# Splitting a weight load whole instead of in halves, in a two-block network on one core

## The chip, the cores and the metric
One core of one Trainium2 chip runs the whole program. The time is the device time of one execution in microseconds (us); a smaller one is better. Engines: TensorE (PE; PEld is its weight loading), VectorE (DVE), ScalarE (ACT), GpSimd (POOL), SyncE (SP, which issues the weight loads).

## What is computed
Two network blocks on 256 tokens of width 2048, in fp32. Cut to its products and stages:
```python
mod = silu(c) @ ada_w + ada_b                       # 96 columns of 128: shifts, scales, gains
h = rmsnorm(x) * (1 + sc1) + sh1
z = h @ w_in                                        # q, k, v, gates, recurrent and merge parts
o_a = compressed, selected and window attention     # 16 heads in 4 groups
o_b = gelu(ly) * rg_lru(conv(lx))
x += g1 * ((sigmoid(ga) * (o_a @ proj_a) + sigmoid(gb) * (o_b @ proj_b)) @ w_out)
x += g2 * ((gelu(conv(gate)) * val) @ ffn_down)     # gate, val = rmsnorm(x).. @ ffn_up
x = rmsnorm(x)
# second block: window attention of 4 head groups, a diagonal state-space scan in 8 rounds,
# a gated unit (w_glu), two projections, merge and output product
```

## The kernel before
**Products in three terms.** Each weight product is done in a reduced form of fp32 three times: high part of the weight with high and with low part of the activation, and low part of the weight with the high one. A weight must therefore be split: `whi` is a rounded copy, made by ScalarE (`split_act`, L1064 to L1069); `wlo` is the weight less `whi`, made by VectorE (`split_dve`, L1071 to L1077), in the place of the raw weight.

**Loads and units.** SyncE loads 1 MB at a time (4 x 128 rows by 512 columns, 2048 elements a partition) into a ring `wraw` of RAW = 5 slots. A load serves two *units* of TensorE, each 24 matmuls of 256 columns (1024 elements a partition of the weight). The table of groups (`groups()`, L52) sets the order of all units; most groups (512 output columns) have 8. The group of the gates alone has one unit and one load, of 768 elements. Between the loads, in the prologue and behind the second and fourth load of many groups up to the first part of the feed-forward stage, stand 96 modulation loads (`ada`): VectorE alone multiplies such a load (L1051) and frees its slot. A weight load's slot is free when TensorE ends its second unit. The ring is filled strictly in order (L1440 to L1458).

**Splits.** `whi` is a ring of HI = 6 halves; a half is made in one instruction on each of the two engines, LEAD = 5 units ahead of its use: at unit u the engines split unit u + 5, and ScalarE waits until TensorE has ended unit u - 1 (L1068). The first eight units are split in the prologue, a load behind each quarter of the first norm.

**Everything else** is written as jobs, generators whose steps all engines walk through in the same order. `walk` (L1413) gives each engine at each unit first its part of the unit (TensorE the matmuls, ScalarE and VectorE the split) and then the steps of the jobs due there. An engine's queue is in order, so a step stands behind the split of its unit. The jobs that matter here: `evac` (L1132, takes a group's result out of PSUM), `nsa` (L413, one head group of the first attention, over the 8 units of the next group; the last over 16), `norm2` (L1298, which stands before the steps of a unit, between two groups), `ssm_tables` (L819), `attention2` (L691, 8 units a head group) and `ssm` (L918, 10 units a round).

The lines that set the lead:
```python
        def unit(g, gr, u, n):
            if FIRST <= u + LEAD < N_UNITS:
                split_dve(dve, u + LEAD)
```
Of the kernel before, what the change touches and what calls it, by code (L numbers as in the profile page):

```python
# [6 lines left out]
F32 = mybir.dt.float32  # L7
F32R = mybir.dt.float32r
ACT = mybir.ActivationFunctionType
ALU = mybir.AluOpType  # L10
AX = mybir.AxisListType

P = 128
# [7 lines left out]
FFC = FF // P  # L21
CB = 512
RAW = 5
HI = 6
LEAD = 5


VEC_SIZES = [("ada_b", 96), ("norm1_g", 16), ("norm2_g", 16), ("final_g", 16), ("norm_w_2", 16),
# [73 lines left out]
def build_program(nc, ctx, xT, vecs, cvec, W, small, outT):  # L102
    base = 16640

    def put(name, at, shape, dt=F32):
        size = 4
        for n in shape[1:]:
            size *= n
        assert base + at + size <= nc.sbuf_usable_end, name
        return nc.alloc_sbuf_tensor_at(name, list(shape), dt, offset=base + at)  # L110
# [4 lines left out]
    K = 1024  # L115


    z0, z1, z2, rM, rW = 0, 32 * K, 64 * K, 96 * K, 112 * K
    rWh = rW + RAW * 8 * K
    rC = rWh + HI * 4 * K  # L120
    rT = rC + 8 * K
    rS = rT + 8 * K
    h1, m1 = put_pair("h1", z0, DC), put_pair("m1", z0, DC)
# [2 lines left out]
    hid = put_pair("hid", z0, 24)  # L126
    res = put("res", rM, [P, DC, T])
    wraw = put("wraw", rW, [P, RAW, 2048])
    wlo = put("wlo", rW, [P, RAW, 2, 1024], F32R)
    whi = put("whi", rWh, [P, HI, 1024], F32R)  # L130
    cb = put("cb", rC, [P, D])
    t1 = put("t1", rT, [P, 4, T])
    t2 = put("t2", rT + 4 * K, [P, 4, T])
# [83 lines left out]
    hi_ready, lo_ready, pe_units, ada_done = sem("hi_ready"), sem("lo_ready"), sem("pe_units"), sem("ada_done")  # L217
# [14 lines left out]
    GR, of = groups()  # L232
    U0, U1 = [], []
# [5 lines left out]
    N_UNITS = at  # L239
    SLOTS, HEAD = [], []  # L240
    unit_slot = {}
    behind = {}
    for g, gr in enumerate(GR):
        for s in range(gr.slots):
            per = gr.units // gr.slots
            if g == 0:
                HEAD.append(range(len(SLOTS), len(SLOTS) + 8))
                SLOTS += [("ada", col + c) for c in range(4 * s, 4 * s + 4) for col in (16, 0)]
            for n in range(per):
                unit_slot[U0[g] + s * per + n] = (len(SLOTS), n)  # L250
            SLOTS.append(("w", g, s, U0[g] + (s + 1) * per))
            for col in gr.ada.get(s, ()):
                behind.setdefault(U0[g] + (s + 1) * per - 1, []).append(len(SLOTS))
                SLOTS.append(("ada", col))
    N_ADA = 0
    ada_no = {}
# [4 lines left out]
    where = []  # L261
# [785 lines left out]
    def ada(dve, z):  # L1047

        slot, col = z % RAW, SLOTS[z][1]
        dve.wait_ge(w_loaded[slot], 16 * (z // RAW + 1))  # L1050
        ve.scalar_tensor_tensor(out=wraw[:, slot, :], in0=wraw[:, slot, :], scalar=1.0, in1=cb[:, :], op0=ALU.mult,  # L1051
                                op1=ALU.mult, accum_out=mod[:, col:col + 1]).then_inc(ada_done, 1)
        if col == 47:
            with_bias(32, 16)
        elif col == 63:
            with_bias(48, 32)
            gain_of(scA, 0, 64, "norm2_g", DC)
        elif col == 95:
            with_bias(80, 16)

    def width(u):
        return 768 if where[u][0].mode == "GATES" else 1024

    def split_act(act, u):  # L1064
        (z, half), r, w = unit_slot[u], u % HI, width(u)
        act.wait_ge(w_loaded[z % RAW], 16 * (z // RAW + 1))
        if u >= HI:
            act.wait_ge(pe_units, u - HI + 1)  # L1068
        sc.activation(whi[:, r, 0:w], wraw[:, z % RAW, 1024 * half:1024 * half + w], ACT.Copy).then_inc(hi_ready, 1)  # L1069

    def split_dve(dve, u):  # L1071
        (z, half), r, w = unit_slot[u], u % HI, width(u)
        dve.wait_ge(hi_ready, u + 1)
        ve.tensor_tensor(wlo[:, z % RAW, half, 0:w], wraw[:, z % RAW, 1024 * half:1024 * half + w],  # L1074
                         whi[:, r, 0:w].bitcast(F32), ALU.subtract).then_inc(lo_ready, 1)
        for z in behind.get(u, ()):
            ada(dve, z)  # L1077

    def split_unit(j, u):
        if j.me == "act":  # L1080
            split_act(j.eng, u)
        if j.me == "dve":
            split_dve(j.eng, u)

    FIRST = 8

    def prologue(j):
        me, ins = j.me, None
        if me == "act":
            j.eng.wait_ge(c_in, 16)  # L1090
            ins = sc.activation(cb[:, :], cb[:, :], ACT.Silu)
        c_ready = j.give("act_to_dve", "act", ins)
        if me == "act":
            j.eng.wait_ge(consts_in, 16)
            sc.activation(ltmp[:, 3, :], V("lru_lambda", 0, DC), ACT.Abs)
            sc.drain()
            ins = sc.activation(ltmp[:, 3, :], ltmp[:, 3, :], ACT.Exp, scale=-1.0)
        j.sync("act_to_dve", "act", "dve", ins)
        if me == "dve":
            j.eng.wait_ge(consts_in, 16)  # L1100
            log_decay()
            ve.tensor_tensor(scB[:, :], V("final_g", 0, DC), V("norm_w_2", 0, DC), ALU.mult)
            ve.drain()
        j.take("act_to_dve", "dve", c_ready)
        for b in range(4):
            if me == "dve":
                for z in HEAD[b]:
                    ada(j.eng, z)
                with_bias(16 + 4 * b, 4)
                with_bias(4 * b, 4)  # L1110
                gain_of(scA, 4 * b, 16 + 4 * b, "norm1_g", 4) if b else None
            if b == 0:
                for _ in norm1(j):
                    pass
                if me == "dve":
                    gain_of(scA, 0, 16, "norm1_g", 4)
            normed(j, "h1", h1, 4 * b, rstd[:, :], scA, 0)
            split_unit(j, 2 * b)
            split_unit(j, 2 * b + 1)

    def merged(j):

# [342 lines left out]
    @block.scalar  # L1465
    def _(act):
        j = Job("act", act)
        prologue(j)

        def unit(g, gr, u, n):  # L1470
            if FIRST <= u + LEAD < N_UNITS:
                split_act(act, u + LEAD)

        walk(j, unit)

    @block.vector
    def _(dve):
        j = Job("dve", dve)
        ve.memset(ones[:, :], 1.0)
        ve.memset(halves[:, :], 0.0)  # L1480
        ve.drain()
        ve.memset(halves[0:64, 0:64], 1.0)
        ve.memset(halves[64:128, 64:128], 1.0)
        ve.drain().then_inc(c_made, 1)
        prologue(j)
        dve.wait_ge(consts_made, 1)

        def unit(g, gr, u, n):
            if FIRST <= u + LEAD < N_UNITS:
                split_dve(dve, u + LEAD)  # L1490

        walk(j, unit)

    @block.tensor
    def _(pe):
        j = Job("pe", pe)
# [2 lines left out]
        pe.wait_ge(consts_made, 1)  # L1499

        def unit(g, gr, u, n):
            r, (z, half) = u % HI, unit_slot[u]
            pair, last = pairs[g % 2], 2 * gr.units - 1
            hi, lo = X[gr.x]
            if n == 0 and g >= 2:
# [2 lines left out]
                pe.wait_ge(S["to_pe"], j.ready[gr.x][-1])  # L1508
            elif n == 0 or (n % 2 == 0 and gr.x not in ("oa", "ob", "at")):
                pe.wait_ge(S["to_pe"], j.ready[gr.x][n // 2])  # L1510
            pe.wait_ge(lo_ready, u + 1)
            wh, wl = whi[:, r, :], wlo[:, z % RAW, half, :]
            terms = lambda k: ((wh, hi[:, k, :]), (wh, lo[:, k, :]), (wl, hi[:, k, :]))
            if gr.mode == "GATES":
                for k in range(DC):
# [108 lines left out]
```

## Time and profile before

| | |
|---|---|
| median of 3 runs | 3038.21 us (3035.32 to 3043.23) |
| profiled execution | 3035.36 us, its span 3033.6 us |
| mean granted TensorE clock | 0.932 of full |
| TensorE busy | 2647.2 us (87%) |
| VectorE busy | 1913.4 us (63%) |
| ScalarE busy | 1126.1 us (37%) |
| GpSimd busy | 164.1 us (5%) |
| chain that ended last, by engine | PE 75%, DVE 14%, DVEq 4%, DMA 4%, ACT 2%, issue 2% |

The span is one execution seen by the profiler; the runs beside it are timed without it. Busy shares are means over stages with different limits: the first attention (about 330 to 600 us), matrix products alone (640 to 2100, with the second norm at 1240), the second norm pair and the tables (2100 to 2260), the second attention (to 2410), the scan (to 2830) and the end. What ended a wait is what counts: the chain of waits is followed back from the last instruction, and "DMA" in it is a load on its way.

### The profile page before, as it was taken

To read this page: it belongs to the slowest core of one execution; us is meant where nothing else is said; L and a number is where in the kernel's file an instruction comes from. 1 tells how busy PE (TensorE), PEld (TensorE's weight loads), DVE (VectorE), ACT (ScalarE), POOL (GpSimd) and SP (SyncE) were. 2 spreads that over 40 slices of the span, in tenths; PEclk is the share of its full clock that TensorE was granted. 3 is DMA by queue.
4 is the path that set the end of the run, shared out by engine and by line. 5 is a ranking of instruction groups with operands and counts; after the bars stand their busy time and mean duration, and the time that the engine had idled before them with its cause. 6 is when DMAs were issued, how large, how long until landed. Compare 5 with 4: busy or idle time off the path is not lost.

```text
span 3033.6 us, 48120 instructions
## 1 busy us (share of the span) xinstructions
PE 2647.2 (87%) x20558; PEld 2570.9 (85%) x20558; DVE 1913.4 (63%) x2538; ACT 1126.1 (37%) x1423; POOL 164.1 (5%) x141
## 2 busy tenths in 40 slices
PE   2499766899999999899999999998898866667899
PEld 2489665899999999899999999998887756666899
DVE  7855444666766565677554555545876687777663
ACT  1122222456533334243443444443444322323332
POOL 0000000000000000000000000000000233332000
PEclk7689888999999999899999999999999978878899
DMA  8765322345677776477555555544543323333454
GB/s 350 279 230 209 129 84 84 125 148 180 235 271 270 280 267 230 156 275 277 197 185 186 183 181 181 183 166 138 177 143 122 119 91 101 104 101 115 153 176 144
DMA packets 237990, 548.20 MB, mean 181 GB/s; under 512 B 10672, under 2 KB 14768, under 8 KB 225360
## 3 DMA queue, kind: packets, MB, share of 16 engines
q1 hardware_dynamic: 233664, 530.31, 50.5%
q0 software_dynamic: 4112, 14.81, 1.4%
q8 instruction: 162, 2.65, 0.3%
q14 instruction: 52, 0.43, 0.0%
HBM read 540.89 MB, written 4.19 MB: 180 GB/s over the span
## 4 chain that ended last, share of the span: by engine, by line
PE 75%; DVE 14%; DVEq 4%; DMA 4%; ACT 2%; issue 2%; PEldq 0%; PEld 0%; ACTq 0%
PE pair L1525 67%; DVE wlo L1074 3%; DMA wraw<-ada_wT_dram 2%; DVE wraw L1051 2%; DMA wraw<-w_in_dram 1%; DVEq L809 1%; PE pair L1531 1%; ACT whi L1069 1%; DVE ssb L812 1%; DVE ssb L810 1%; DVE ssb L815 1%; DVEq L814 1%; PE bank L390 1%; PE bank L566 1%; DVE ssb L808 1%
## 5 line engine op out<-in xcount | busy, mean ns | idle before, releaser
L1074 DVE TENSOR_TENSOR wlo<-wraw,whi 128x1024 fp32r<-128x1024 f32 x809 | 997.7, 1245 | 874.2 <-ACT whi L1069 852.0
L1069 ACT ACTIVATE whi<-wraw 128x1024 fp32r<-128x1024 f32 x809 | 844.5, 1057 | 1632.9 <-PE pair L1525 950.4
L1525 PE MATMUL pair<-h_hi,whi 128*128 128x256 f32 x4128 | 1208.0, 293 | 171.1 <-DVE wlo L1074 90.3
L1525 PE MATMUL pair<-h_lo,whi 128*128 128x256 f32 x4128 | 1192.8, 289 | 0.0
L1525 PE MATMUL pair<-h_hi,wlo 128*128 128x256 f32 x4128 | 1190.6, 288 | 0.0
L1525 PEld LDWEIGHTS pair<-h_hi,whi 128*128 128x128 f32 x4128 | 818.9, 198 | 190.5 <-issue 117.6
L1525 PEld LDWEIGHTS pair<-h_lo,whi 128*128 128x128 f32 x4128 | 819.1, 198 | 0.5
L1525 PEld LDWEIGHTS pair<-h_hi,wlo 128*128 128x128 f32 x4128 | 817.5, 198 | 0.0
L1051 DVE SCALAR_TENSOR_TENSOR wraw<-wraw,cb 128x2048 f32<-128x2048 f32 x96 | 218.7, 2287 | 28.8 <-DMA wraw<-ada_wT_dram 27.7
L1525 PE MATMUL pair<-hid_hi,whi 128*128 128x256 f32 x768 | 218.5, 284 | 0.0
L1525 PE MATMUL pair<-hid_lo,whi 128*128 128x256 f32 x768 | 217.3, 283 | 0.0
L1525 PE MATMUL pair<-hid_hi,wlo 128*128 128x256 f32 x768 | 217.3, 283 | 0.0
L1525 PEld LDWEIGHTS pair<-hid_lo,whi 128*128 128x128 f32 x768 | 147.4, 192 | 0.2
L1525 PEld LDWEIGHTS pair<-hid_hi,whi 128*128 128x128 f32 x768 | 147.4, 192 | 0.2
L1525 PEld LDWEIGHTS pair<-hid_hi,wlo 128*128 128x128 f32 x768 | 147.4, 192 | 0.0
L1525 PE MATMUL pair<-m_hi,whi 128*128 128x256 f32 x512 | 145.5, 284 | 0.0
L1525 PE MATMUL pair<-m_lo,whi 128*128 128x256 f32 x512 | 144.9, 283 | 0.0
L1525 PE MATMUL pair<-m_hi,wlo 128*128 128x256 f32 x512 | 144.9, 283 | 0.0
L1525 PEld LDWEIGHTS pair<-m_lo,whi 128*128 128x128 f32 x512 | 98.3, 192 | 0.1
L1525 PEld LDWEIGHTS pair<-m_hi,whi 128*128 128x128 f32 x512 | 98.3, 192 | 0.1
L1525 PEld LDWEIGHTS pair<-m_hi,wlo 128*128 128x128 f32 x512 | 98.3, 192 | 0.0
L1525 PE MATMUL pair<-oa_hi,whi 128*128 128x256 f32 x256 | 72.4, 283 | 0.0
(391 smaller groups left out, 3131.5 us busy)
## 6 DMA issues: line engine op xcount, KB each, us to landing
wraw<-w_in_dram SPq DMA_DIRECT2D x172, 1024.0 KB, 5.2
wraw<-ada_wT_dram SPq DMA_DIRECT2D x96, 1024.0 KB, 5.3
wraw<-ffn_up_dram SPq DMA_DIRECT2D x96, 1024.0 KB, 5.0
wraw<-ffn_down_dram SPq DMA_DIRECT2D x48, 1024.0 KB, 5.0
wraw<-w_out_dram SPq DMA_DIRECT2D x32, 1024.0 KB, 5.1
wraw<-proj_a_dram SPq DMA_DIRECT2D x16, 1024.0 KB, 6.8
wraw<-proj_b_dram SPq DMA_DIRECT2D x16, 1024.0 KB, 6.2
wraw<-w_attn_proj_dram SPq DMA_DIRECT2D x8, 1024.0 KB, 5.0
```

Of the source, the lines that this page charges most:

```text
L390: ins = te.matmul(bank[1][:, 0, 0:60], wcmp[:, l, :], blocks[:, l, :], start=(l == 0), stop=(l == 31))
L566: te.matmul(bank[3][:, 0, :], vv(br, 0), pt[:, br, 0:T], start=False, stop=False, skip_group_check=True)
L808: en.tensor_tensor(y, a_im, b_im, ALU.mult)
L809: en.drain()
L810: en.tensor_tensor(o_re, x, y, ALU.add if conj else ALU.subtract)
L812: en.tensor_tensor(x, a_re, b_im, ALU.mult)
L814: en.drain()
L815: last = en.tensor_tensor(o_im, x, y, ALU.subtract if conj else ALU.add)
L1051: ve.scalar_tensor_tensor(out=wraw[:, slot, :], in0=wraw[:, slot, :], scalar=1.0, in1=cb[:, :], op0=ALU.mult, op1=ALU.mult, accum_out=mod[ ...
L1069: sc.activation(whi[:, r, 0:w], wraw[:, z % RAW, 1024 * half:1024 * half + w], ACT.Copy).then_inc(hi_ready, 1)
L1074: ve.tensor_tensor(wlo[:, z % RAW, half, 0:w], wraw[:, z % RAW, 1024 * half:1024 * half + w], whi[:, r, 0:w].bitcast(F32), ALU.subtract).t ...
L1525: ins = te.matmul(pair[:, o, :], w[:, at_w + o * P:at_w + (o + 1) * P], x, start=(k == 0 and o % 2 == 0 and t == 0), stop=(k == last and t ...
```

## The change
A split now takes a whole load. `whi` is a ring of 3 loads (the same memory as 6 halves), both engines make 2048 elements in one instruction, and the semaphores of the splits count loads. The lead is two loads: at the first unit of load L the engines split load L + 2, if it is not among the first four, and ScalarE waits until TensorE has ended load L - 1. At the second unit there is no split. TensorE waits at each unit for its load's split. The modulation product that stood behind the split of a load's second half stands behind that of the load; the ring of raw loads, the order of the loads and what frees their slots are unchanged. The gates' load is 768 elements wide as before.
```diff
--- before.py
+++ after.py
@@ -21,8 +21,7 @@
 FFC = FF // P
 CB = 512
 RAW = 5
-HI = 6
-LEAD = 5
+HI = 3
 
 
 VEC_SIZES = [("ada_b", 96), ("norm1_g", 16), ("norm2_g", 16), ("final_g", 16), ("norm_w_2", 16),
@@ -117,7 +116,7 @@
 
     z0, z1, z2, rM, rW = 0, 32 * K, 64 * K, 96 * K, 112 * K
     rWh = rW + RAW * 8 * K
-    rC = rWh + HI * 4 * K
+    rC = rWh + HI * 8 * K
     rT = rC + 8 * K
     rS = rT + 8 * K
     h1, m1 = put_pair("h1", z0, DC), put_pair("m1", z0, DC)
@@ -126,8 +125,8 @@
     hid = put_pair("hid", z0, 24)
     res = put("res", rM, [P, DC, T])
     wraw = put("wraw", rW, [P, RAW, 2048])
-    wlo = put("wlo", rW, [P, RAW, 2, 1024], F32R)
-    whi = put("whi", rWh, [P, HI, 1024], F32R)
+    wlo = put("wlo", rW, [P, RAW, 2048], F32R)
+    whi = put("whi", rWh, [P, HI, 2048], F32R)
     cb = put("cb", rC, [P, D])
     t1 = put("t1", rT, [P, 4, T])
     t2 = put("t2", rT + 4 * K, [P, 4, T])
@@ -250,7 +249,7 @@
                 unit_slot[U0[g] + s * per + n] = (len(SLOTS), n)
             SLOTS.append(("w", g, s, U0[g] + (s + 1) * per))
             for col in gr.ada.get(s, ()):
-                behind.setdefault(U0[g] + (s + 1) * per - 1, []).append(len(SLOTS))
+                behind.setdefault(sum(1 for slot in SLOTS if slot[0] == "w") - 1, []).append(len(SLOTS))
                 SLOTS.append(("ada", col))
     N_ADA = 0
     ada_no = {}
@@ -1058,31 +1057,40 @@
         elif col == 95:
             with_bias(80, 16)
 
-    def width(u):
-        return 768 if where[u][0].mode == "GATES" else 1024
-
-    def split_act(act, u):
-        (z, half), r, w = unit_slot[u], u % HI, width(u)
+    LOADS = [z for z, slot in enumerate(SLOTS) if slot[0] == "w"]
+    load_at = {z: n for n, z in enumerate(LOADS)}
+
+    def width(n):
+        return 768 if GR[SLOTS[LOADS[n]][1]].mode == "GATES" else 2048
+
+    def split_act(act, n):
+        z, w = LOADS[n], width(n)
         act.wait_ge(w_loaded[z % RAW], 16 * (z // RAW + 1))
-        if u >= HI:
-            act.wait_ge(pe_units, u - HI + 1)
-        sc.activation(whi[:, r, 0:w], wraw[:, z % RAW, 1024 * half:1024 * half + w], ACT.Copy).then_inc(hi_ready, 1)
-
-    def split_dve(dve, u):
-        (z, half), r, w = unit_slot[u], u % HI, width(u)
-        dve.wait_ge(hi_ready, u + 1)
-        ve.tensor_tensor(wlo[:, z % RAW, half, 0:w], wraw[:, z % RAW, 1024 * half:1024 * half + w],
-                         whi[:, r, 0:w].bitcast(F32), ALU.subtract).then_inc(lo_ready, 1)
-        for z in behind.get(u, ()):
-            ada(dve, z)
-
-    def split_unit(j, u):
+        if n >= HI:
+            act.wait_ge(pe_units, SLOTS[LOADS[n - HI]][3])
+        sc.activation(whi[:, n % HI, 0:w], wraw[:, z % RAW, 0:w], ACT.Copy).then_inc(hi_ready, 1)
+
+    def split_dve(dve, n):
+        z, w = LOADS[n], width(n)
+        dve.wait_ge(hi_ready, n + 1)
+        ve.tensor_tensor(wlo[:, z % RAW, 0:w], wraw[:, z % RAW, 0:w], whi[:, n % HI, 0:w].bitcast(F32),
+                         ALU.subtract).then_inc(lo_ready, 1)
+        for a in behind.get(n, ()):
+            ada(dve, a)
+
+    def split_load(j, n):
         if j.me == "act":
-            split_act(j.eng, u)
+            split_act(j.eng, n)
         if j.me == "dve":
-            split_dve(j.eng, u)
-
-    FIRST = 8
+            split_dve(j.eng, n)
+
+    FIRST = 4
+
+    def next_split(u):
+
+        z, n = unit_slot[u]
+        n_load = load_at[z] + 2
+        return n_load if n == 0 and FIRST <= n_load < len(LOADS) else None
 
     def prologue(j):
         me, ins = j.me, None
@@ -1115,8 +1123,7 @@
                 if me == "dve":
                     gain_of(scA, 0, 16, "norm1_g", 4)
             normed(j, "h1", h1, 4 * b, rstd[:, :], scA, 0)
-            split_unit(j, 2 * b)
-            split_unit(j, 2 * b + 1)
+            split_load(j, b)
 
     def merged(j):
 
@@ -1468,8 +1475,8 @@
         prologue(j)
 
         def unit(g, gr, u, n):
-            if FIRST <= u + LEAD < N_UNITS:
-                split_act(act, u + LEAD)
+            if next_split(u) is not None:
+                split_act(act, next_split(u))
 
         walk(j, unit)
 
@@ -1486,8 +1493,8 @@
         dve.wait_ge(consts_made, 1)
 
         def unit(g, gr, u, n):
-            if FIRST <= u + LEAD < N_UNITS:
-                split_dve(dve, u + LEAD)
+            if next_split(u) is not None:
+                split_dve(dve, next_split(u))
 
         walk(j, unit)
 
@@ -1499,7 +1506,8 @@
         pe.wait_ge(consts_made, 1)
 
         def unit(g, gr, u, n):
-            r, (z, half) = u % HI, unit_slot[u]
+            z, half = unit_slot[u]
+            r = load_at[z] % HI
             pair, last = pairs[g % 2], 2 * gr.units - 1
             hi, lo = X[gr.x]
             if n == 0 and g >= 2:
@@ -1508,8 +1516,8 @@
                 pe.wait_ge(S["to_pe"], j.ready[gr.x][-1])
             elif n == 0 or (n % 2 == 0 and gr.x not in ("oa", "ob", "at")):
                 pe.wait_ge(S["to_pe"], j.ready[gr.x][n // 2])
-            pe.wait_ge(lo_ready, u + 1)
-            wh, wl = whi[:, r, :], wlo[:, z % RAW, half, :]
+            pe.wait_ge(lo_ready, load_at[z] + 1)
+            wh, wl = whi[:, r, 1024 * half:], wlo[:, z % RAW, 1024 * half:]
             terms = lambda k: ((wh, hi[:, k, :]), (wh, lo[:, k, :]), (wl, hi[:, k, :]))
             if gr.mode == "GATES":
                 for k in range(DC):
```
What this moves, at three places. Names: `wlo`, `whi` the low and high parts, `sm...` score tiles, `st` and `ltmp` the softmax's small vectors. Line numbers of the changed kernel differ by 1 to 7.

VectorE in the first head group of the first attention, from the end of the first score shift to the split before the first head's result, before:
```order
L495 TENSOR_SCALAR st<-st 128x4
L1074 TENSOR_TENSOR wlo<-wraw,whi 128x1024
L506 RECIPROCAL st<-st 128x4
L509 TENSOR_TENSOR st<-st,gates 128x4
...
L495 TENSOR_SCALAR st<-st 128x4
L1074 TENSOR_TENSOR wlo<-wraw,whi 128x1024
L310 CAST oa_hi<-bank 128x256
```
and now:
```order
L494 TENSOR_SCALAR st<-st 128x4
L505 RECIPROCAL st<-st 128x4
L508 TENSOR_TENSOR st<-st,gates 128x4
...
L494 TENSOR_SCALAR st<-st 128x4
L1076 TENSOR_TENSOR wlo<-wraw,whi 128x2048
L309 CAST oa_hi<-bank 128x256
```
The half that stood before the first head's softmax weights has moved behind them and behind the second score shift, into the split that stood there.

VectorE in the fourth head group of the second attention, from the last head's score shift to its softmax weights, before:
```order
L722 TENSOR_TENSOR ltmp<-vec,ltmp 128x2
L1074 TENSOR_TENSOR wlo<-wraw,whi 128x1024 x2
L732 TENSOR_TENSOR ltmp<-ltmp 128x2
L734 RECIPROCAL ltmp<-ltmp 128x2
L736 TENSOR_SCALAR sm20B<-sm20B,ltmp 128x128
```
and now:
```order
L721 TENSOR_TENSOR ltmp<-vec,ltmp 128x2
L1076 TENSOR_TENSOR wlo<-wraw,whi 128x2048
L731 TENSOR_TENSOR ltmp<-ltmp 128x2
L733 RECIPROCAL ltmp<-ltmp 128x2
L735 TENSOR_SCALAR sm20B<-sm20B,ltmp 128x128
```
Two halves, of the sixth and of the seventh unit, have become one whole, of the seventh.

VectorE in the scan's first round, between the four scans and the second complex product, before:
```order
L983 SCALAR_TENSOR_TENSOR ssb_119<-ssp,ssb_121 128x256
L1074 TENSOR_TENSOR wlo<-wraw,whi 128x1024
L807 TENSOR_TENSOR ssb_122<-ssb_116,ssb_118 128x512
L808 TENSOR_TENSOR ssb_123<-ssb_117,ssb_119 128x512
L810 TENSOR_TENSOR ssb_120<-ssb_122,ssb_123 128x512
```
and now:
```order
L982 SCALAR_TENSOR_TENSOR ssb_119<-ssp,ssb_121 128x256
L806 TENSOR_TENSOR ssb_122<-ssb_116,ssb_118 128x512
L807 TENSOR_TENSOR ssb_123<-ssb_117,ssb_119 128x512
L809 TENSOR_TENSOR ssb_120<-ssb_122,ssb_123 128x512
```
The split of the fourth unit is gone from there; the whole one stands before the first complex product, at the third unit.

## Rows read from the trace of the kernel before

**Rows 1.** Busy time in windows of 100 us: engines' busy us (instructions), PEclk, DMA share, GB/s
```profile
400.00:500.00 100.00, 67.40 (x427) 60.73 (x426) 45.50 (x101) 26.46 (x60) 0.00 (x0) 0.85 0.27 95
...
1600.00:1700.00 100.00, 100.00 (x836) 100.00 (x835) 47.16 (x47) 36.87 (x35) 0.00 (x0) 1.00 0.54 179
```
**Rows 2.** The page's costliest groups: busy, mean ns; the third: one line's instruction durations
```profile
L1074 DVE TENSOR_TENSOR wlo<-wraw,whi 128x1024 fp32r<-128x1024 f32 x809 | 997.7, 1245 | 874.2 <-ACT whi L1069 852.0
L1069 ACT ACTIVATE whi<-wraw 128x1024 fp32r<-128x1024 f32 x809 | 844.5, 1057 | 1632.9 <-PE pair L1525 950.4
...
L1091 ACT ACTIVATE cb<-cb x1: 1909/1909/1909, 5.7 to 5.7; 128x2048 f32<-128x2048 f32 x1
```
**Rows 3.** VectorE in order of time, prologue: start, us, line, tiles, [idle before <-releaser]
```profile
49.70 2.29 DVE L1051 SCALAR_TENSOR_TENSOR wraw<-wraw,cb 128x2048 f32<-128x2048 f32 x1
...
51.91 2.29 DVE L1051 SCALAR_TENSOR_TENSOR wraw<-wraw,cb 128x2048 f32<-128x2048 f32 x1
...
132.64 8.15 DVE L1074 TENSOR_TENSOR wlo<-wraw,whi 128x1024 fp32r<-128x1024 f32 x7
```
**Rows 4.** First attention: last exponential on ScalarE, then chain of waits (start, us, what)
```profile
353.75 0.19 ACT L501 ACTIVATION_READ_ACCUMULATOR sm<-sm,st 128x1 f32 x1
...
358.12 4.85 DMA wraw<-w_in_dram
...
362.99 1.06 ACT whi L1069
...
364.08 1.23 DVE wlo L1074
...
368.31 4.69 PE pair L1525 x24
...
380.93 3.65 PE pair L1525 x24
```
**Rows 5.** TensorE in order of time, first attention: first and last of three such waits
```profile
366.77 0.48 PE L546 MATMUL bank<-ident,sm 128*128 128x128 f32 x1 [8.68 <-DVE sm L514]
...
517.11 0.47 PE L546 MATMUL bank<-ident,sm 128*128 128x128 f32 x1 [8.79 <-DVE sm L514]
```
**Rows 6.** Chain of waits, end of the first head group
```profile
399.39 5.01 DMA wraw<-w_in_dram
...
416.27 2.98 PE pair L1525 x24
```
**Rows 7.** Chain of waits, before the second norm
```profile
1237.82 4.94 DMA wraw<-ffn_up_dram
```
**Rows 8.** Order of time at the state-space tables: VectorE, then TensorE
```profile
2218.00 2.59 DVE L1074 TENSOR_TENSOR wlo<-wraw,whi 128x1024 fp32r<-128x1024 f32 x2
...
2219.28 0.58 PE L1525 MATMUL pair<-h_hi,whi 128*128 128x256 f32 x1 [3.30 <-DVE wlo L1074]
```
**Rows 9.** Order of time in the second attention: VectorE and TensorE
```profile
2326.25 1.23 DVE L1074 TENSOR_TENSOR wlo<-wraw,whi 128x1024 fp32r<-128x1024 f32 x1 [0.74 <-ACT whi L1069]
...
2328.46 0.33 PE L768 MATMUL bank<-ident,sm20B 128*128 128x128 f32 x1 [1.45 <-DVE sm2B L737]
...
2334.08 1.23 DVE L1074 TENSOR_TENSOR wlo<-wraw,whi 128x1024 fp32r<-128x1024 f32 x1
```
**Rows 10.** Order of time in a round of the scan: VectorE and TensorE
```profile
2510.88 1.96 DVE L1074 TENSOR_TENSOR wlo<-wraw,whi 128x1024 fp32r<-128x1024 f32 x1 [0.33 <-issue]
...
2528.66 1.22 DVE L1074 TENSOR_TENSOR wlo<-wraw,whi 128x1024 fp32r<-128x1024 f32 x1 [1.13 <-ACT whi L1069]
...
2536.68 1.23 DVE L1074 TENSOR_TENSOR wlo<-wraw,whi 128x1024 fp32r<-128x1024 f32 x1
...
2563.95 0.58 PE L1525 MATMUL pair<-h_hi,whi 128*128 128x256 f32 x1 [9.87 <-DVEq L302]
```
**Rows 11.** Order of time beside the modulation loads: issue by SyncE, ScalarE's split
```profile
904.34 0.92 SPq L1458 DMA_DIRECT2D wraw<-proj_a_dram  x2
...
910.76 2.01 ACT L1069 ACTIVATE whi<-wraw 128x1024 fp32r<-128x1024 f32 x2 [7.65 <-DMA wraw<-proj_a_dram]
```

## The prediction

> **What bounds the kernel now.** I read the stretches first. Where only matrix products run, TensorE is full: 835 matmuls in 100 us, so the 24 matmuls of a unit (half a load) take 2.87 us; in the first attention only 427 ran in 100 us [rows 1]. Next came the costs of the two halves of a split [rows 2, 3], then, place by place, what TensorE waits for and the chain behind it [rows 4 to 11]. The profiled execution took 3035.36 us, 2.85 below the median of the runs shown; the sum is made against 3035.36 and 2.85 is added at the end. About 0.3%, 9 us, is what a measurement of this kernel can tell from no change.
>
> **Prices.** A half split costs ScalarE 1.06 us and VectorE 1.245 [rows 2]. No whole split is in the trace. For ScalarE I take the one activation of 2048 elements, 1.91 us [rows 2]. For VectorE I take the modulation products of the same width, which start 2.21 us apart; seven half splits back to back took 8.15 us, so they start 1.15 apart [rows 3]. Two halves thus hold VectorE for some 2.28 us and one whole for 2.21: over 404 loads 28 us of an engine that is idle a third of the time, and near nothing where it is not. The bounds are 0 (width costs all) and 0.20 a load (2 x 1.245 - 2.287). So the instruction count is not the matter; the order is. Call the first unit of a load even, the second odd.
>
> The second half of load L was split at even unit 2(L-2) and stays there. The first half, split one odd unit earlier, moves there. At odd units both engines have no split any more; at even ones a split ends 0.85 (ScalarE) plus 1.07 (VectorE) = 1.92 us later, and the steps behind it wait. Buffers hold six halves as before, and slots are freed by whole loads as before, so the DMA issues keep their order.
>
> **Gain: waits for a load.** In stages with modulation columns between the loads, a slot comes free only when TensorE ends the odd unit at which the load's first half was due. VectorE and ScalarE stood before a DMA with the steps of that odd unit behind them.
> - First kind, three times (before 366.77, 441.79, 517.11): unit ends and load is issued at 358.12, DMA 4.85, ScalarE to 364.05, VectorE to 365.3, and only then the softmax weights that TensorE waited 8.68 us for; the next unit ran at the low clock, 4.69 instead of 2.87 [rows 4, 5]. Now the weights and the next score shift run before the load lands (the exponentials that they need ended at 353.94). TensorE goes on at 358.1: transposes about 1, unit 2.9, products 2.7, at 364.7. Load landed at 363.0, plus 1.91, 2.21 and the 2.9 us of steps that stand between split and transposes: it waits until 370.1, 5.4 us. Then transposes and unit, clock low, 6.2: 376.3, against 384.58 before (380.93 + 3.65) [rows 4]. That is 8.2 each, 24.6 in all. The ends are 10.7 each, if the clock stays high, and 5.
> - Second kind, twice: unit ends at 399.39, DMA 5.01, then the half splits, with TensorE waiting behind them; the next head group's first products ended at 416.27 [rows 6]. Now the last head is finished during the DMA, but the whole split (1.91 + 2.21) and the eviction behind it (1.2) still stand before the next head group: about 410.7 for its start, and then a slow start. I take 2.5 each, 5 in all (1 to 4.5).
> - Before the second norm a unit ended and a load was issued at 1237.82; with DMA 4.94, 1.06 and 1.23 its half split was done at 1245.0, while TensorE's last two units ended at 1237.82 + 2 x 2.87 = 1243.6 [rows 7]. It moves behind the norm: 1.4.
>
> **Cost: the shorter lead.**
> - State-space tables: VectorE is the bound, TensorE has run ahead until its splits are used up and restarts at 2219.28, when the split that starts at 2218.00, of an odd unit, is done [rows 8]. Now the even unit before it hangs on the same place: TensorE stops one unit earlier, 2.87, and the split takes 1.07 more: 3.9, and about 1 for a clock that falls in a wait of 7 us. 5 (1 to 7).
> - Second attention, four head groups. Before the last head's weights at the seventh (even) unit stand ScalarE's split, behind the exponentials, and VectorE's (2326.25, which waited for ScalarE's); TensorE waits 1.45 us for them at 2328.46 [rows 9]. At the sixth unit nothing is saved, as that time was idle. So 0.85 + 1.07 = 1.9, four times, and 1.07 three times at the start of the next group (split at 2334.08 straight before its first copy) [rows 9]: 10.8, and 2 for the clock: 13 (8 to 20).
> - Scan, eight rounds of ten units. At the third unit ScalarE must wait for TensorE, then split, then VectorE split (2528.66), then the complex products: 1.9 later. The fourth unit has no split (2536.68 goes): 1.14 back. At the fifth, 0.3 more, as a split beside GpSimd's work costs 1.96 instead of 1.22; at the seventh and eighth +1.07 and -1.14. 1.0 a round, all on the chain, since TensorE waits for it at the end (9.87 us before 2563.95) [rows 10]: 8 (0 to 15).
> - Small ones: the half that TensorE waited for behind 132.64 [rows 3] is a whole now, +1.1; the compression step behind it drops about 1 of VectorE's splits, -1; the first head group and the gated unit each have a longer even split before their evictions, +0.8 and +1. Together +1.9.
> - Steady stages: nothing, TensorE covers it. The tightest is beside the modulation loads: issued 904.34, ScalarE starts 910.76, plus 1.91 and 2.21 is 914.9; TensorE needs it four units after 904.34, at 915.9 [rows 11]. One us of cover. A load landing 2 us later would cost 1, 16 such places: end of the range 5.
>
> Sum: -24.6 - 5 - 1.4 + 5 + 13 + 8 + 1.9 = -3.1. 3035.36 - 3.1 + 2.85 = **3035 us**, chance 0.47.
>
> **The rivals.**
> 1. The clock comes back with the waits (0.22). The three first-kind waits give 10.7 each and the second kind 4.5 each, and the costs stay at their lower half (tables 4, attention 9, scan 4): -32 - 9 - 1.4 + 4 + 9 + 4 + 1.9 = -23.5, 3015. For it: the low clock doubled a unit's time after 8.68 us idle [rows 4]. Against: 5.4 us of wait are left at each.
> 2. The shorter lead wins, slower (0.20). In the second block, where no split ever waited for a load, every even unit puts 1.9 us before VectorE's steps and the odd ones give nothing back, since TensorE's unit covers them: scan 8 x 1.9 = 15, second attention 20, tables 7. With the gains as forecast: -31 + 42 + 1.9 = +13, 3051. It decides once the scan round grows by 2 us or more.
> 3. Fewer instructions (0.08). If each load freed 0.20 us of VectorE also back to back, the some 60 loads from tables to scan, where it is the bound, would give 12: 3035 - 12 = 3023. The Trainium skill (VectorE: DVE Perf Modes, the section on the TRN2 errata) says that each SBUF-source instruction pays a fixed extra latency and that one large tile pays it once, many small ones each time; by that rule this rival would be right. The starts 1.15 and 2.21 apart [rows 3] say that back to back little of it is left to save.
> 4. The change of order does nothing, because the same engines wait for the same TensorE units (0.03): 3038.
>
> **How the numbers follow.** The forecast's own range is 3024 to 3047; of its 0.47, 0.08 fall under 3029, 0.35 within 9 us and 0.04 above. Rival 1 gives 0.19 faster and 0.03 same, rival 2 0.17 slower and 0.03 same, rival 3 0.05 faster and 0.03 same, rival 4 same. Faster 0.32, same 0.47, slower 0.21. The range takes in most of rivals 1 and 2: 3014 to 3054.
>
> **What would show it.** After: 404 splits of 2048, near 1.91 us on ScalarE and 2.29 on VectorE. In the first attention TensorE's waits of 8.7 us gone, one of some 5 before the second head's transposes, and the span up to 600 us shorter by about 28. From 2130 to 2850 some 25 longer: waits of 3.4 us in place of 1.45 before each fourth head's transposes, a wait of some 7 us near 2220, scan rounds of 54 instead of 53.2. No wait of TensorE for a split from 640 to 1230 and 1260 to 2100. I am wrong if a whole split costs more than 2.5 us or much less than 2.2, if TensorE waits in the steady stages, or if the attention's gain is under 15.

## The result, and the profile after

The change made the kernel slower: 3073.56 us (3070.49 to 3077.84, 4 runs) against 3037.57 (3035.32 to 3043.23, 4 runs), ratio 1.0117, 95% interval 1.0097 to 1.0136. The forecast was 3035 with a range of 3014 to 3054: the time lies 38.6 us above the one and 19.6 above the end of the other. The profiled execution took 3071.8 us, its span 3070.1.

**Where the time went.** VectorE runs the same instructions in the same order in both kernels, but for the splits. So the start of one and the same VectorE instruction in the two traces gives the time gained or lost up to it. The marks are instructions of VectorE at 325.35 us of the trace before (the modulation product ahead of the first attention), 596.92, 1259.73 (the second norm), 1476.83 (behind the modulation products), 2260.02 (the second attention's first copy), 2411.26 (the scan) and 2837.03. In the change they start at 336.75, 580.91, 1239.51, 1483.07, 2268.30, 2438.83 and 2871.65. From mark to mark, in us:

| stage (time of before) | forecast | measured |
|---|---|---|
| start to 325 | +0.9 | +11.4 |
| 325 to 597, first attention | -29.6 | -27.4 |
| to 1260, recurrent part, merge, second norm | -1.4 | -4.2 |
| to 1477, feed-forward with modulation loads | 0 | **+26.5** |
| to 2260, down products, tables | +5 | +2.0 |
| to 2411, second attention | +13 | +19.3 |
| to 2837, scan | +8 | +7.1 |
| to the end | +1 | +1.8 |
| span | -3.1 | +36.4 |

The costliest groups of the page after, which answer to [rows 2]: busy us, mean ns | idle before them:
```profile
L1076 DVE TENSOR_TENSOR wlo<-wraw,whi 128x2048 fp32r<-128x2048 f32 x405 | 937.8, 2318 | 910.5 <-ACT whi L1071 899.7
...
L1071 ACT ACTIVATE whi<-wraw 128x2048 fp32r<-128x2048 f32 x405 | 773.6, 1911 | 1296.5 <-PE pair L1533 797.1
```
The prices were right: 1.91 and 2.32 us. VectorE is busy 1857.8 us in place of 1913.4, and the kernel is slower: its busy time was not what mattered.

**The first attention** did what was forecast. The chain of waits at its first head group (start, us, what), which answers to [rows 4]:
```profile
370.50 5.06 DMA wraw<-w_in_dram
...
375.57 1.92 ACT whi L1071
...
377.52 2.29 DVE wlo L1076
...
383.46 4.08 PE pair L1533 x24
```
and TensorE in order of time [idle before <- releaser], which answers to [rows 5]:
```profile
382.27 0.33 PE L545 MATMUL bank<-ident,sm0B 128*128 128x128 f32 x1 [4.85 <-DVE smB L513]
```
One wait of 4.85 us (forecast 5.4) stands where there were 8.68 and others. The unit behind it still ran slowly, 4.08 us in place of 2.87.

**The feed-forward stage** is where the forecast failed. Windows between the marks, before, then after: engines' busy us (instructions), PEclk, DMA share, GB/s:
```profile
1259.73:1476.83 217.10, 217.10 (x1797) 217.10 (x1798) 160.88 (x180) 89.01 (x99) 0.00 (x0) 0.99 0.72 254
```
```profile
1239.51:1483.07 243.56, 226.17 (x1816) 225.30 (x1817) 158.44 (x143) 84.45 (x62) 0.00 (x0) 0.97 0.65 229
```
TensorE was always busy there before. Now it waits five times, 17.4 us together by the table of waits. The first wait has a cause of its own: the whole split stands behind the last step of the second norm. The other four are alike; the first, the second and the third wait in order of time:
```profile
1256.16 0.36 PE L1533 MATMUL pair<-h_hi,whi 128*128 128x256 f32 x1 [3.56 <-DVE wlo L1076]
...
1295.74 0.36 PE L1533 MATMUL pair<-h_hi,whi 128*128 128x256 f32 x1 [3.30 <-DVE wlo L1076]
...
1345.39 0.55 PE L1533 MATMUL pair<-h_hi,whi 128*128 128x256 f32 x1 [3.35 <-DVE wlo L1076]
```
The chain of waits that leads to the third:
```profile
1324.10 1.92 ACT whi L1071
...
1326.05 2.29 DVE wlo L1076
...
1328.42 0.03 ACT t L1184
...
1330.35 1.81 ACT whi L1071
...
1336.69 1.57 DVE t L659 x4
...
1340.06 0.02 ACT t L1192
...
1341.03 1.90 ACT whi L1071
...
1342.96 2.30 DVE wlo L1076
...
1345.39 4.66 PE pair L1533 x25
```
This reads: whole split on ScalarE, on VectorE, evacuation (L1184), the next whole split on both, the convolution on VectorE (L659), the gelu on ScalarE (L1192), and only behind it the split that TensorE needs at 1342.04. Its load was issued at 1330.56 and had long landed. The two splits ahead of the convolution are each handed on whole, ScalarE to VectorE and VectorE to the next, and the split itself hands nothing to TensorE before 1345.26.

In the kernel before, at the same place, the load was issued at 1342.05 and ScalarE began its first half as soon as it had landed, ahead of the gelu:
```profile
1347.23 1.06 ACT L1069 ACTIVATE whi<-wraw 128x1024 fp32r<-128x1024 f32 x1 [5.28 <-DMA wraw<-ffn_up_dram]
```
The loss of the stage is more than its waits. TensorE's unit behind the third wait takes 4.5 us (the 4.66 above are 25 products); the units behind the first, fourth and fifth are slow as well, and the one behind the second, after 3.30 us, is not. The four slow units cost 1.4 to 1.6 us each, some 6 in all. The last 2 to 3 us of the 26.5 come from the mark itself, as TensorE has done 19 products more (1816 against 1797) when VectorE reaches it.

**Smaller places.** The second attention's last heads wait 3.71 and 3.38 us (forecast 3.4; 1.45 before, [rows 9]), but its clock is 0.92 where it was 0.96. The tables' wait is 8.28 us (forecast 7):
```profile
2223.57 0.55 PE L1533 MATMUL pair<-h_hi,whi 128*128 128x256 f32 x1 [8.28 <-DVE wlo L1076]
...
2300.14 0.33 PE L767 MATMUL bank<-ident,sm20B 128*128 128x128 f32 x1 [3.71 <-DVE sm2B L736]
...
2343.73 0.33 PE L767 MATMUL bank<-ident,sm20B 128*128 128x128 f32 x1 [3.38 <-DVE sm2B L736]
```
**The start** loses 11.4 us, of which the forecast had 0.9. Each of TensorE's four waits for the first splits is 22.7 to 23.0 us where it was 21.7 to 21.8: 4.4 us in all, where I had counted the fourth alone. The rest comes out of this chain:
```profile
147.16 1.93 ACT whi L1071
...
149.11 2.29 DVE wlo L1076
...
151.41 1.13 DVEq L1169
...
152.94 1.86 POOL wcmp L375
154.81 12.39 DMA w<-cmp_w_k_dram
167.20 0.14 issue
167.34 13.60 PE bank L389 x64
```
ScalarE's whole split waits for TensorE's unit to end at 147.10, the evacuation stands behind it, GpSimd behind that, and the compression's own weights land after TensorE wants them (3.00 us). The 64 products then take 13.60 us; before, without a wait ahead of them, they took 7.33. That is 9.3 us together. Some 4 of them come back at the next products of the compression, for which TensorE waited 5.3 us before and waits 1.1 now.

### The profile page after: what moved, and what is told of

Read it like the earlier page. It is cut to its first block, busy times and chain, and to the rows that moved or that the text cites. A ratio compares the mean times of both kernels' runs of the same rounds, so it can differ in the third digit from the quotient of the medians.

```text
span 3070.1 us, 46918 instructions
## 1 busy us (share of the span) xinstructions
PE 2664.1 (87%) x20558; PEld 2586.7 (84%) x20558; DVE 1857.8 (61%) x2134; ACT 1059.6 (35%) x1019; POOL 171.4 (6%) x141
## 4 chain that ended last, share of the span: by engine, by line
PE 68%; DVE 15%; DVEq 6%; DMA 4%; ACT 4%; issue 2%; PEldq 0%; SPq 0%; POOL 0%; PEld 0%; ACTq 0%
PE pair L1533 61%; DVE wlo L1076 4%; ACT whi L1071 3%; DMA wraw<-ada_wT_dram 2%; DVEq L808 1%; DVE wraw L1050 1%; DMA wraw<-w_in_dram 1%; PE pair L1539 1%; DVE ssb L811 1%; DVE ssb L809 1%; DVE ssb L806 1%; DVE ssb L814 1%; DVEq L813 1%; PE bank L389 1%; DMA wraw<-ffn_up_dram 1%
## 5 line engine op out<-in xcount | busy, mean ns | idle before, releaser
L1076 DVE TENSOR_TENSOR wlo<-wraw,whi 128x2048 fp32r<-128x2048 f32 x405 | 937.8, 2318 | 910.5 <-ACT whi L1071 899.7
L1071 ACT ACTIVATE whi<-wraw 128x2048 fp32r<-128x2048 f32 x405 | 773.6, 1911 | 1296.5 <-PE pair L1533 797.1
L1050 DVE SCALAR_TENSOR_TENSOR wraw<-wraw,cb 128x2048 f32<-128x2048 f32 x96 | 218.8, 2288 | 21.3 <-DMA wraw<-ada_wT_dram 20.2
```

Of the source, the lines that this page charges most:

```text
L1071: sc.activation(whi[:, n % HI, 0:w], wraw[:, z % RAW, 0:w], ACT.Copy).then_inc(hi_ready, 1)
L1076: ve.tensor_tensor(wlo[:, z % RAW, 0:w], wraw[:, z % RAW, 0:w], whi[:, n % HI, 0:w].bitcast(F32), ALU.subtract).then_inc(lo_ready, 1)
```

## The experiments

All kernels from here on are made from the change, with a plan in place of its fixed rule. For each load the plan says in what parts each engine splits it, and at which unit. The plan goes by a *policy*: "W" is the change (one whole split, at the first unit of the load two ahead); "E" is the kernel before (two halves, each five units ahead); "L" is late halves (two halves of 1024, each signalled alone, both at the unit where "W" splits); "O" is a whole split one unit earlier than in "W". A policy can be set for each stage in which a split is made: P the start, A the first attention, B to the output product, C the feed-forward products with modulation loads, D the rest of that part, E tables, F second attention, G scan, H the end. "E" in all stages would be the kernel before, but for waits around the load of the gates, which takes a whole place of the ring. The kernels that have "E" at the start lose 3 to 5 us there; that this is the reason is not shown.

The unit at which load n is split (`us` are the load's units):
```python
        if k == "E":
            at_u = us[part[1]] - 5
        elif k == "O":
            at_u = units_of[n - 3][-1]
        else:
            at_u = units_of[n - 2][0]
```
A part is written (half, elements, count): the semaphore rises by count units at its end. All use the ring of three loads. They were measured in four batches, in which the kernel before took 3035.9, 3037.9, 3038.4 and 3038.4 us, so differences of medians across batches are good to some 3 us. The stages are those of one profiled execution, in us against the profiled one of the kernel before, from the same marks (C is the column to 1477; "C+" to 2260):

| kernel | median | start | att. 1 | to 1260 | C | C+ | att. 2 | scan | end |
|---|---|---|---|---|---|---|---|---|---|
| the change | 3073.6 | +11.4 | -27.4 | -4.2 | +26.5 | +2.0 | +19.3 | +7.1 | +1.8 |
| late_halves | 3007.7 | +0.6 | -31.9 | -4.1 | +3.3 | +2.4 | +10.9 | -8.0 | -1.5 |
| late_buffer | 3033.3 | +9.2 | -28.2 | -3.7 | +4.7 | +2.1 | +12.3 | +2.4 | -0.3 |
| joined_halves | 3093.8 | +9.5 | -20.2 | -3.0 | +31.0 | +3.9 | +22.1 | +10.9 | +1.8 |
| act_whole | 3077.3 | +12.6 | -20.9 | -4.0 | +19.3 | +2.8 | +17.6 | +9.1 | +1.7 |
| dve_whole | 3067.6 | +6.1 | -22.9 | -3.6 | +31.9 | +1.8 | +16.9 | +1.7 | -0.4 |
| ffn_early | 3061.3 | +11.5 | -21.4 | -2.0 | +3.2 | +3.6 | +20.6 | +9.1 | +1.7 |
| ffn_late | 3062.4 | +12.6 | -18.9 | -2.0 | +7.9 | +3.4 | +20.6 | +9.0 | +1.7 |
| whole_early | 3328.2 | +29.6 | +66.2 | +35.3 | +2.1 | +22.2 | +70.1 | +63.0 | +6.2 |
| att1_late_halves | 3001.6 | +3.1 | -34.6 | -2.1 | -0.2 | -0.2 | 0.0 | -0.1 | 0.0 |
| att1_whole | 3011.2 | +4.4 | -24.5 | -3.5 | -0.3 | -0.3 | 0.0 | -0.1 | 0.0 |
| mixed | 2993.1 | +2.9 | -34.5 | -2.2 | -0.2 | -0.2 | -0.1 | -6.8 | -1.4 |
| mixed_down_whole | 2999.2 | +4.8 | -28.2 | -2.3 | +2.2 | -2.7 | -0.2 | -6.8 | -1.4 |

**late_halves: order without width.** Policy "L" in all stages, in place of "W":
```diff
-    parts = [(0, width(n), len(us))]
+    parts = [(0, 1024, 1), (1, 1024, 1)]
```


> Halves of 1024 as before, each signalled alone, but both made at the first unit of the load two ahead: the change's order without its width. If the order is the cause: 3060 to 3072 us (the change's 3073.6 less up to 1 us at each wait, since TensorE may start on the first half), first attention some 28 us shorter than before, feed-forward products with modulation loads some 20 to 26 longer, second attention and scan some 25 longer. If the width is the cause: 3038 within 6, and none of these.

Measured: 3007.72 us, ratio 0.9899 (0.9879 to 0.9918). Neither theory: the order alone is a *gain* of 28 to 30 us, and the whole split costs 66 on top of it. The order costs in the second attention (+10.9), gives in the first (-31.9) and in the scan (-8.0), and takes 3.3 in the stage where the change lost 26.5. There the same place reads, ScalarE, then VectorE:
```profile
1318.07 3.89 ACT L1136 ACTIVATE whi<-wraw 128x1024 fp32r<-128x1024 f32 x4
```
```profile
1319.14 4.63 DVE L1145 TENSOR_TENSOR wlo<-wraw,whi 128x1024 fp32r<-128x1024 f32 x4 [2.12 <-ACT whi L1136]
```
The load was issued at 1309.29, and TensorE needs its split four units of 2.87 us later, at 1320.8 by this estimate. The gelu, at 1317.10, comes 7.8 us after the issue, where in the change it comes 9.5 after. From ScalarE's start to the first low half at 1320.4 it is 2.3 us; in the change it is 4.2 (1341.03 to 1345.26). These two differences, 1.7 and 1.9 us, make up the change's wait of 3.35 us: here the half is 0.4 us early.

**whole_early.** Policy "O" everywhere: `at_u = units_of[n - 3][-1]`.

> Whole splits as in the change, but at the odd unit before (the last of the load three ahead), ahead of the steps of that unit: the change's width in nearly the old order. With a ring of three ScalarE must there wait until TensorE ends that unit. If the order is the cause: the feed-forward stretch is as before (26 us shorter than the change's), the first attention's gain of 28 is gone and each of its waits is 2 us longer than before; the second block is worse than both by ScalarE's wait, 10 to 40 us; together 3080 to 3120. If the width is the cause: every stage as in the change, 3074.

Measured: 3328.21 us, 1.0953 (1.0932 to 1.0975). The feed-forward stage came out as the order theory says (+2.1), but the first attention became 66 us longer and the total was 208 us over the expected upper end. (86 of VectorE's steps stand in another order here; the marks are the same instructions.) ScalarE now waits at every odd unit until TensorE ends it, and everything behind it waits too. ScalarE in order of time, second attention:
```profile
2422.77 1.91 ACT L1136 ACTIVATE whi<-wraw 128x2048 fp32r<-128x2048 f32 x1 [14.92 <-PE pair L1598]
...
2454.84 1.92 ACT L1136 ACTIVATE whi<-wraw 128x2048 fp32r<-128x2048 f32 x1 [7.51 <-PE pair L1598]
```
Why C alone was spared is not shown; I argue that the steps there have no products of their own for TensorE.

**att1_late_halves, ffn_early.** Policy "E" with A = "L"; policy "W" with C = "E".

> The kernel before, only that in the first attention (loads split from the q groups to the first ly) both halves are made at the even unit. If the order is the cause: the stretch to 600 us ends 24 to 30 us earlier, nothing else moves, 3010 us (3005 to 3016), faster than both. If the gain comes from the width: 3038.

> The change, only that in the feed-forward products with modulation loads (gate and val, i under 4, first half) the halves are made as before, the first one an odd unit earlier. If the order there is the cause of the loss that the forecast lacked: 26 us shorter than the change, 3047 (3043 to 3052), and no wait of TensorE for a split between 1260 and 1450. If it is something else (DMA, clock): 3074.

Measured: att1_late_halves 3001.55 (0.9883, 0.986 to 0.9907), 34 us below the kernel before and 3.5 below the expected range, and little moved behind it (-2.1 in the next stage). ffn_early: 3061.3 (1.0071, 1.0045 to 1.0097), 9 over its expected range; its stage C is 23.3 us shorter than the change's, but the first attention, with the same instructions as in the change, was 6 longer.

**The parts of a whole split.** All three split at the unit where the change does. joined_halves has `parts = [(0, 1024, 0), (1, 1024, 2)]` on both engines; act_whole keeps the halves on VectorE and has `act_parts = [(0, 2048, 2)]` on ScalarE; dve_whole the reverse.

> Late halves again, two instructions of 1024 on each engine, but each pair is signalled once, at its end, as a whole split is. If what costs is that nothing can start on the first half: the change's time or up to 12 us over it (one more fixed start a load), 3074 to 3086. If what costs is an instruction 2048 elements long: 3008, as late_halves.

> Late halves, but ScalarE makes the high part whole, in one instruction; VectorE in halves, each signalled alone. Handing-on theory: VectorE starts 0.85 us later than in late_halves, TensorE may start on the first half 3.15 us after the split begins, where late_halves takes 2.3 and the change 4.2. So some 45% of the change's loss against late_halves (66 us): 3037 (3020 to 3050). Instruction theory: half of it, for whichever engine is the cause.

> Late halves, but VectorE makes the low part whole; ScalarE in halves, each signalled alone. VectorE needs both halves before it starts and TensorE has nothing before VectorE's whole is done, as in the change. Handing-on theory: the change's time, 3074 (3068 to 3084). If ScalarE's long instruction was the cause: 3010 to 3020.

Measured: joined_halves 3093.84 (1.0183, 1.0167 to 1.0198), 8 us beyond the expected end; act_whole 3077.3 (1.0128, 1.0107 to 1.0149), where 3020 to 3050 was expected; dve_whole 3067.61 (1.0096, 1.0075 to 1.0117), at the lower end of what handing-on would give and far from 3020. The long instruction is thus not the cause: two of 1024 signalled together cost 20 us more than one of 2048. What a whole split waits for and hands on is: joined_halves is 86 us over late_halves with the same instructions in the same places. But my proportion for act_whole was wrong. In part that is because it left the ring out: ScalarE may start a whole only when both halves of its place are free, and TensorE frees them 2.87 us apart. Measured alone below, that is 25.5 us; added to the 3037 it still leaves 15 us.

**late_buffer: that wait alone.** late_halves, but for ScalarE's wait; in effect:
```diff
-            act.wait_ge(pe_units, (us[-1] if cnt != 1 or half else us[0]) + 1)
+            act.wait_ge(pe_units, us[-1] + 1)
```


> late_halves with one wait more: ScalarE's first half, too, starts only when both halves of its place in the ring are free, as a whole split must; each half is still signalled alone. It prices that part of the whole split by itself. If the buffer is a good part of the loss (as act_whole, which has it, lost 69 us against late_halves, though VectorE hands on halves there): 3035 to 3060. If the handing-on alone is the cause: 3008 to 3015.

Measured: 3033.25 (3019.36 to 3038.41, 10 runs; 0.9981, 0.9965 to 0.9996), just under the 3035 to 3060 expected and 25.5 us over late_halves. Its runs spread over 19 us, those of late_halves over 3, so the 25.5 is the least certain of the prices here. ScalarE in the third round of the scan, in late_halves and in the change:
```profile
2507.92 1.06 ACT L1136 ACTIVATE whi<-wraw 128x1024 fp32r<-128x1024 f32 x1 [0.92 <-PE pair L1598]
2510.80 1.06 ACT L1136 ACTIVATE whi<-wraw 128x1024 fp32r<-128x1024 f32 x1 [1.82 <-PE pair L1598]
2513.68 1.06 ACT L1136 ACTIVATE whi<-wraw 128x1024 fp32r<-128x1024 f32 x1 [1.82 <-PE pair L1598]
```
```profile
2558.01 1.92 ACT L1071 ACTIVATE whi<-wraw 128x2048 fp32r<-128x2048 f32 x1 [0.52 <-PE pair L1533]
2563.77 1.92 ACT L1071 ACTIVATE whi<-wraw 128x2048 fp32r<-128x2048 f32 x1 [3.84 <-PE pair L1533]
```
Halves start each 2.88 us, as TensorE frees them; a whole starts each 5.76. By stage the buffer costs in the start (8.6 of the change's 11.4: late_buffer shows the same late compression weights, a wait of 0.87 us and 11.64 us for the 64 products) and in the scan (+10.4), and next to nothing in C (+1.4). A ring of four loads, which would take this wait away, was not tried.

act_whole is late_buffer with ScalarE's two halves made as one, so that VectorE starts 0.85 us later. It costs 44 us more (3077.3 against 3033.3), 14.6 of them in C: TensorE's five waits there are 12.6 us together, where late_buffer has two, 2.5 together.

The prices do not simply add up. dve_whole has everything handed on whole to TensorE, but ScalarE's halves become free and are filled one by one; it costs 60 us over late_halves. From there to the change, which adds the wait for a whole place and saves an instruction of ScalarE for each load, it is 6 us (3067.6 to 3073.6). The wait for the whole place is worth 25.5 us where halves are handed on, and much less where they are not.

**ffn_late.** Policy "W" with C = "L".

> The change, with late halves, each signalled alone, in the feed-forward products with modulation loads and nowhere else: there the order of the change stays and only the whole split goes (ffn_early undid both). If the whole split is the cause of the 26 us lost there: some 23 less than the change, 3050 (3046 to 3056). If the order is: 3074.

Measured: 3062.43 (1.0083, 1.0066 to 1.01), 11 below the change where 23 was expected. The profiled execution was the longest of its four runs, 3069.63, and in it stage C came down from +26.5 to +7.9, as expected but for 4 us; what was lost again is mostly in the first attention (8.5), which has the same instructions in both kernels. Windows from mark to mark, the change, then ffn_late:
```profile
336.75:580.91 244.16, 191.83 (x1264) 175.83 (x1263) 131.05 (x277) 81.67 (x183) 0.00 (x0) 0.90 0.31 108
```
```profile
337.92:590.55 252.63, 197.01 (x1262) 181.68 (x1261) 131.21 (x277) 81.54 (x183) 0.00 (x0) 0.86 0.30 104
```
The same work took 244.2 us, at a granted clock of 0.90, and 252.6, at 0.86.

**mixed, mixed_down_whole, att1_whole.** Policy "E" with A, B, G, H = "L"; the same with D = "W"; "E" with A = "W".

> Halves everywhere, each signalled alone; late in the first attention, the recurrent and merge stages, the scan and the end, early elsewhere. By the stages of late_halves and att1_late_halves: 34 less in the first attention, 2 in the next stages, 8 in the scan, 1.5 at the end: 3036 - 45 = 2991 (2985 to 3000), faster than all before it.

> The kernel mixed, with whole splits in the stages where TensorE always runs (the rest of the first feed-forward part after the modulation loads, and both down products, 1475 to 2107 us in the kernel before). Both theories: TensorE covers it there, 2993 as mixed (2989 to 2999). If a whole split costs wherever it stands: over 3000.

> The kernel before, with whole splits in the first attention alone, the one place where the forecast saw a gain. By the change's own stages the stretch to 607 us gives 27 us back, a few more than halves would leave: 3037 - 27 = 3010 (3006 to 3016), against 3002 with late halves there.

Measured: mixed 2993.1 (0.9856, 0.9841 to 0.987), 1.4% below the kernel before and the fastest of all. att1_whole 3011.18 (0.9911, 0.9892 to 0.993). mixed_down_whole 2999.19, at the upper end of what was expected (2999), but its D stages are where they were in mixed (+2.2 - 2.7 together); the 6 us lie in the first attention again, at a clock of 0.87 in place of 0.91, and 1.9 in the start. A whole split cost nothing in these stages, where TensorE never waits for a split.

## Why the prediction was wrong

Point by point, by its own steps.
- *Prices of a whole split*: right (1.91 and 2.2 to 2.3 us), and so was "the instruction count is not the matter" for the total. But it has a size: joined_halves against the change gives 20 us for one instruction less on each engine and load. Rival 3 (12 us) had a true mechanism; it was outweighed. The Trainium skill (VectorE: DVE Perf Modes, the section on the TRN2 errata) says that one large tile pays a fixed latency once that many small ones pay each time. The 20 us agree with it in sign.
- *"The order is" the matter, at no cost for the width*: this is the step that failed. The prediction priced a whole split by its duration, 1.92 us later at the even unit, and not by what two halves hand on. late_halves has the same order and comes to 3007.7. One way from the one kernel to the other, in measured medians: 3037.6 before, -29.85 for the order (late_halves), +25.5 for waiting until a whole place in the ring is free (late_buffer), +60.6 for handing on whole (joined_halves), -20.3 for fewer instructions (the change): 3073.6. These are the prices in this order of steps; in another they come out otherwise (dve_whole). The forecast priced the move and the longer instructions together at -3.1. It had a wait for the ring in the scan alone, and nothing for what a first half lets begin.
- *"Steady stages: nothing, TensorE covers it"*: here that step failed most, 0 for 26.5; it alone is two thirds of the 39.5 us between the forecast -3.1 and the measured +36.4. The tightest place had been looked for beside the merge stage's modulation loads [rows 11], where ScalarE started 6.4 us after the issue. In the feed-forward stage it started 10.5 us after (1330.56 to 1341.03), since the gelu and two whole splits stand ahead; in the kernel before it had started 5.2 after (1342.05 to 1347.23), ahead of the gelu. I read one period of one stage and took it for all 16. The end of the range for this term, 5, had been worked out from a late DMA, which did not come.
- *First attention*: -29.6 forecast, -27.4 measured, and the wait it named is there (4.85 for 5.4). Two slips in its working did no harm: 399.39 + 5.01 + 1.91 + 2.21 + 1.2 is 409.7 and not 410.7, and the low clock did not double the unit's time, as rival 1 says, but made 4.69 us of 2.87. *Second norm*: -1.4 for -4.2 in a stage that holds more than it.
- *Second attention*: the waits right to 0.3 us, the term too small (13 for 19.3). TensorE's busy time grew from 134.0 to 140.4 us, at a clock of 0.92 for 0.96, and 2 had been allowed for that. *Tables*: 5 forecast, 2.0 measured for the stretch, within its ends. *Scan*: 8 for 7.1, but not for the reason given: its order alone gives 8.0 us back (late_halves), where a cost of 1.0 a round was forecast for it, and the ring (10.4) and the handing on (4.7 more, fewer instructions counted in) take it away.
- *Start*: 0.9 for 11.4. One of four equal waits was counted, and the transfer of the compression weights, issued by GpSimd behind an evacuation behind the split, was not looked at.
- *Rival 2*, "the shorter lead wins, slower", was right in its sign, but by luck: its second block came to 28 where it said 42 and the forecast's own terms said 26, and the time is above its 3051 because of the steady stages, which it too had at nothing, and the start.

## What to carry to other kernels

A producer's two half-size pieces are not only two instructions: each is a signal on which the next engine starts, and each frees a place in a ring by itself. Before merging them, count at every stage what the first piece alone lets begin, and how much later the merged one can start. Move and merge are separate edits: here the move alone gained 1% and the merging took 2.2% away. And check cover in each stage that has steps of its own, not in the one that looks tightest for the DMA.

## What was not expected of the hardware

- A short wait of TensorE can cost more than its length. Of the change's five waits in the feed-forward stage, of 3.28 to 3.90 us, four were followed by a unit that took 1.4 to 1.6 us longer than the usual, and one, of 3.30 us, was not. In act_whole, with waits of 2.3 to 2.9 us at the same places, it was two of five. So the cost comes in steps and is not in proportion, and a single wait does not tell whether it will be paid.
- The same instructions in the first attention took 244.2 and 252.6 us, at granted clocks of 0.90 and 0.86, in two kernels that differ only later and that had started the stage 1.2 us apart. They were measured in different batches, and the runs of one kernel differ too (ffn_late: 3061.1 to 3069.6), so it is not shown that the kernels are the reason. It limits what a single profile says of that stage to some 8 us.
